# Two transformer blocks on one core: the first block's attention bias built by VectorE and GpSimd together

## What is computed

```python
def swa_bias_and_mask(positions, rel_bias):
    bucket = t5_bucket(pq[..., :, None] - pk[..., None, :])     # 32 buckets
    bias = rel_bias[bucket].astype(jnp.float32).reshape(b, nb, WINDOW, 2 * WINDOW, SWA_KV_HEADS, SWA_GROUP)
    ...

scores = jnp.einsum('bnqhgd,bnkhd->bnqkhg', qb, kk).astype(jnp.float32) * (SWA_HEAD_DIM ** -0.5) + bias
scores = jnp.where(mask, scores, NEG_INF)
```

## Time and profile before

| what | value |
|---|---|
| median of 3 runs | 2380.89 us (2378.52 to 2381.33) |
| the profiled execution | 2379.98 us |
| its span, from the first to the last instruction | 2378.1 us |
| PE, DVE, ACT, POOL busy | 2193.1, 991.6, 532.3, 3.6 us |
| granted clock of PE, mean | 0.968 of full speed |
| DVE busy in the first 250 us | 222 us |

### The profile page before, as it was taken

The page is one execution under the profiler, slowest core; times in us unless marked ns, Lnnn a source line. Parts: engine busy times, 40 slices in busy tenths (PEclk is TensorE's granted clock), DMA queues, the critical chain, the costliest instruction groups (busy, mean ns, idle before and its releaser), DMA issues.

```text
span 2378.1 us, 30893 instructions
## 1 busy us (share of the span) xinstructions
PE 2193.1 (92%) x12840; PEld 1510.0 (63%) x12840; DVE 991.6 (42%) x2028; ACT 532.3 (22%) x963; POOL 3.6 (0%) x11
## 2 busy tenths in 40 slices
PE   7999889998999889997999899999997799999996
PEld 6877579997877679997987644334334544334333
DVE  7899535552158335557447512111112511111112
ACT  2112104430113204334234211111112211111111
POOL 0000000000000000000000000000000000000000
PEclk9999999999999999998999899999999899999999
DMA  6445633453445733442220799999996399999993
GB/s 254 154 165 212 280 144 140 149 190 130 169 177 213 307 117 142 166 186 99 107 83 25 287 425 428 428 428 428 428 428 291 128 424 428 429 428 429 428 427 158
DMA packets 43770, 621.95 MB, mean 262 GB/s; under 512 B 4864, under 2 KB 4864, under 8 KB 5664
## 3 DMA queue, kind: packets, MB, share of 16 engines
q1 hardware_dynamic: 34416, 489.94, 50.9%
q10 hardware_dynamic: 8640, 125.83, 12.4%
q0 software_dynamic: 624, 4.92, 0.5%
HBM read 619.62 MB, written 1.05 MB: 261 GB/s over the span
## 4 chain that ended last, share of the span: by engine, by line
PE 64%; DMA 21%; DVE 11%; issue 2%; ACT 1%; SPq 0%; ACTq 0%; DVEq 0%
PE bank L549 19%; PE bank L1136 11%; DMA ring<-in_experts 11%; DMA arena<-in_experts 10%; PE bank L1158 4%; DVE wide L1729 3%; PE bank L742 3%; PE bank L743 3%; PE bank L744 3%; PE sums L744 3%; PE sums L743 3%; PE sums L742 3%; PE sums L549 2%; PE bank L870 2%; DVE arena L1756 2%; PE bank L871 2%
## 5 line engine op out<-in xcount | busy, mean ns | idle before, releaser
L549 PE MATMUL bank<-h,ring 128*128 128x256 f32 x1600 | 358.4, 385 | 15.1 <-DVE h L1654 12.1
L549 PEld LDWEIGHTS bank<-h,ring 128*128 128x128 f32 x1600 | 306.1, 193 | 65.0 <-DVE h L1654 12.9
L1158 PE MATMUL bank<-ring,wide 128*64 128x512 f32 x1024 | 233.8, 598 | 0.0
L2383 DVE TENSOR_TENSOR wide<-bank,wide 128x256 f32<-128x256 f32 x64 | 27.2, 425 | 420.1 <-ACT wide L1551 420.1
L1952 DVE TENSOR_TENSOR ring_split<-ring,arena_split 128x2048 fp32r<-128x2048 f32 x64 | 143.8, 2288 | 110.6 <-ACT arena_split L1387 110.5
L2391 DVE SCALAR_TENSOR_TENSOR scratch_split<-bank,small,wide_split 128x512 fp32r<-128x512 f32 x64 | 48.0, 750 | 272.3 <-ACT wide_split L1563 272.3
L742 PE MATMUL bank<-h_split,arena_split 128*128 128x256 f32 x512 | 146.7, 286 | 15.0 <-DVE ring_split L1952 15.0
L743 PE MATMUL bank<-scratch_split,arena_split 128*128 128x256 f32 x512 | 146.3, 286 | 0.0
L744 PE MATMUL bank<-h_split,ring_split 128*128 128x256 f32 x512 | 146.3, 286 | 0.0
L742 PE MATMUL sums<-smax_split,arena_split 128*128 128x256 f32 x512 | 144.9, 283 | 0.0
L743 PE MATMUL sums<-smax_split,arena_split 128*128 128x256 f32 x512 | 144.9, 283 | 0.0
(11 more groups left out here) (331 smaller groups left out, 3468.3 us busy)
## 6 DMA issues: line engine op xcount, KB each, us to landing
ring<-in_stream SPq DMA_DIRECT2D x100, 2048.0 KB, 7.8
ring<-in_experts SPq DMA_DIRECT2D x98, 2048.0 KB, 22.9
arena<-in_experts SPq DMA_DIRECT2D x34, 2048.0 KB, 24.3
ring<-in_experts ACTq DMA_DIRECT2D x30, 2048.0 KB, 14.1
arena<-in_experts ACTq DMA_DIRECT2D x30, 2048.0 KB, 14.0
wide<-in_na_bias POOLq DMA_DIRECT2D x1, 1536.0 KB, 8.6
arena<-in_consts POOLq DMA_DIRECT2D x1, 1088.0 KB, 5.3
x<-in_tokens SPq DMA_DIRECT2D x1, 1024.0 KB, 6.3
```

Of the source, the lines that this page charges most:

```text
L549: mm = pe.matmul(dst, a, b, start=(first and i == 0), stop=(i == len(terms) - 1))
L1158: mm = pe.matmul(banks[2][64 * half:64 * half + 64, :], M["turned"][:, e % 2, at:at + 64], w[:, k, 512 * half:512 * half + 512], start=(k ...
```

## The change

DVE keeps heads 0, 4, 1 and 5, the ones used in units 8 to 11. POOL builds heads 2, 6, 3 and 7, used in units 12 to 15, in this order, each head through all its 31 steps before the next. POOL has no fused multiply-add in this code: a step is a comparison times delta into `scratch` 4 or 5, then an addition to the head, each waiting for the instruction before. POOL begins when DVE has seeded all heads (`bias_begun`), and DVE waits, ahead of the scores of a unit whose head is POOL's, for that head's last addition (`bias_built`). The comparison of each step stays on DVE as well.

```diff
+VECTOR_HEADS, POOL_HEADS = (0, 4, 1, 5), (2, 6, 3, 7)
...
+            S.wait(pool, "bias_begun", 0)
+            for hd in POOL_HEADS:
+                v = flat2(wbias[:, hd])
+                for b in range(1, N_BUCKETS):
+                    step = scratch[:, 4 + S.count.get("bias_built", 0) % 2, :]
+                    if S.count.get("bias_built", 0) > 1:
+                        pool.wait_ge(S.sem("bias_built"), S.count["bias_built"] - 1)
+                    S.give(pool.tensor_scalar(step, flat2(A["away"]), float(thresholds[b - 1]), A["delta"][:, b * HEADS + hd:b * HEADS + hd + 1],
+                                              ALU.is_ge, ALU.mult), "bias_step", hd, b)
+                    S.wait(pool, "bias_step", hd, b)
+                    if b > 1:
+                        S.wait(pool, "bias_built", hd, b - 1)
+                    S.give(pool.tensor_tensor(v, v, step, ALU.add), "bias_built", hd, b)
             S.wait(pool, "x_added", 1, "mlp")
...
                 for hd in range(HEADS):
                     v = flat(wbias[:, hd])
                     ins = dve.tensor_scalar(v, v, A["delta"][:, hd:hd + 1], None, ALU.add)
-                link(ins)
...
+                give_link(ins, "bias_begun", 0)
...
-                    for hd in range(HEADS):
+                    for hd in VECTOR_HEADS:
                         v = flat(wbias[:, hd])
                         ins = dve.scalar_tensor_tensor(out=v, in0=reached, scalar=A["delta"][:, b * HEADS + hd:b * HEADS + hd + 1],
                                                        in1=v, op0=ALU.mult, op1=ALU.add)
...
                     hd = sink_of(u)
+                    if l == 0 and hd in POOL_HEADS:
+                        S.wait(dve, "bias_built", hd, N_BUCKETS - 1)
```

More of the change, by code:

```diff
@@ L378, in two_blocks_kernel @@
         loggam = small[:, 0:8]
+        thresholds = bucket_thresholds()
         def norm_col(i, s, which, k):
@@ L1714, in first_steps @@
                     ins = dve.tensor_scalar(v, v, A["delta"][:, hd:hd + 1], None, ALU.add)
-                link(ins)
-            thresholds = bucket_thresholds()
+                give_link(ins, "bias_begun", 0)
             steps = iter(range(1, N_BUCKETS))
```

## The result

The changed kernel is slower: median 2439.23 us of 4 runs (2435.69 to 2451.73) against 2380.26, a ratio of 1.0243 (95% interval 1.0212 to 1.0274), or +58 us. Its profiled execution took 2435.69 us, +55.7 against that of before.

What follows compares the result with a forecast made beforehand. DVE and PE were taken to run neck and neck. POOL's 109 us less 28 in free time put 81 on DVE; minus 49 saved, +32 on 2379.98 gave 2412.0 us, whole range 2375 to 2455.

Steps and rivals of the forecast that it cites:

- the forecast's mechanism: While POOL builds bias, its instructions and DVE's two-operand ones take full turns; +32 us at unit 8, kept to the end.
- The ledger of PE and DVE: Layer 0, units 8 to 15: 49 us less on DVE move the end by only 3.3 us, if nothing else changes.
- the fixed taps: Twelve convolution taps per unit from unit 8 on, with the softmax, keep DVE at 7.83 us a unit.
- The coupling: Up to unit 8: of POOL's 109 us, 28 fit free DVE time, 81 fall on DVE; less 49 saved, +32 us.
- PE's waits for DVE between 113 and 194 us: Sign of the forecast: such waits appear in that stretch if turns are taken, none before the change.
- The threshold of 0.20 us a POOL instruction: Loss on DVE per POOL instruction, over 248 of them, at which the 49 us removed are used up.
- The price of a POOL step: One head's comparison (0.33 us) and addition (0.55) on POOL: 0.88 us, bounds 0.66 to 1.30, about 1.1 with waits.
- "near 224" with turns: Sign: POOL's end is near 224 us under the forecast, 170 without coupling, 264 if DVE goes first.
- the due pace of 1.70 us: POOL's 124 steps, last due at unit 15 at 245.2 us, leave 211.3 / 124 = 1.70 us a step.
- POOL alone too slow: Rival, chance 0.04: POOL late from 1.70 us a step; at 2.2 head 7 is 62 us behind, +58, 2438 us.
- DVE goes first: Rival, chance 0.10: POOL only gets gaps, DVE isn't slowed, head 7 is late ahead of unit 15; +15.5, 2395.5 us.
- No coupling: Rival, chance 0.29: POOL's work costs DVE nothing that matters, DVE waits for PE before unit 9; -3.3, 2376.7 us.

Runs made afterwards that it cites:

- two runs without a wait: Changed kernel with only heads 3 and 7 on POOL: 1.0023, +5.5 us; changed kernel with POOL's comparison replaced by product and sum with constants: 1.0033, +7.9 us.
- two-head run: Changed kernel with only heads 3 and 7 on POOL and six heads on DVE: ratio 1.0023, +5.5 us (+2.9 to +8.1).
- full-DVE run: Kernel before, DVE with all eight heads, plus POOL's 248 instructions beside it on spare tiles: ratio 1.0287, +68 us.

## Why the prediction was right or wrong

- **Direction and range** held: slower, 2439 in 2375 to 2455. The direction rests on the forecast's mechanism, for the kernel is slower by coupling alone too (+5.5 and +7.9 in the two runs without a wait). That the size came out near is partly luck: the point, 2412, was 27 us short, and most of the +58 came from a wait that the forecast didn't have.
- **The ledger of PE and DVE** held. 49 us off DVE were worth 5.0 (3.3 forecast, in the interval), and the named cap, the fixed taps, was the cap: moved forward, the gain is 11.
- **The coupling** was right in kind and too high in size. 81 us were to fall on DVE by unit 8; 33 did, and 52 in all. Two terms were off. The loss is 0.45 us a step to unit 8, and 0.54 with DVE full all the time, under the 0.65 that 81 / 124 makes (0.44 an addition and 0.13 a comparison when each runs alone). And at its real pace POOL had made some 73 of its 124 steps by unit 8, so it went on taking time from DVE in units 8 to 14. At unit 8 the changed kernel stood at +0, where +32 was forecast, and PE's waits for DVE between 113 and 194 us, a sign named for the forecast, did not come. The threshold of 0.20 us a POOL instruction was the useful number: the pair costs 0.27.
- **The price of a POOL step is the term that failed.** Taken 0.88 us, bounds 0.66 to 1.30, from memsets, and about 1.1 with the waits; measured 1.86 with nothing beside it, and 2.05 with the waits. The addition was 0.72 against my 0.55, near enough. The comparison was 1.14 against 0.33. I costed an instruction by the elements it passes, with a row of another operation, and on POOL the operation is the price. My upper bound took half the memset's rate, and its 0.75 for the addition doesn't follow from that: two operands in turn at 1.67 ns an element make 0.97, and the bound 1.52. Even so it lies under 1.86, since the comparison lasts more than three times the 0.33 of one pass. So POOL's end, "170" alone and "near 224" with turns, became 303, and the due pace of 1.70 us, worked out correctly, was missed by every step.
- **The rival "POOL alone too slow"** at 2.2 us a step gave 2438 and had a chance of 0.04. It was the mechanism of the end: DVE's 18.9 us of coupling lie under POOL's 270 us, and without them DVE would only have waited longer, for a POOL that needs until 287 by itself. Counted from the seeding, 2.05 us a step makes POOL some 40 us late, and the 0.13 us by which DVE slows its step add 16: together the 55.7 of the two executions. It should have had several times that chance: the pace stood at 1.1 against 1.70 on rows of an operation that was not the added one.
- **DVE goes first** is refuted: beside additions turns are one for one, and DVE is the one that waits. **No coupling** is refuted by the two-head run (+5.5, interval above nought) and by the full-DVE run.
- The trace agrees with the rule named from the Trainium skill, SBUF — State Buffer, section Who interferes with whom, in who disturbs whom: two-operand DVE instructions beside POOL reads, one-operand fast ones beside memsets too, two-operand ones not beside memsets (475 to 486 ns). The size does not agree: that section says "for the whole instruction" of the two-port modes, and the prediction took it for two-operand instructions too; an addition of 0.72 to 0.79 us would then hold DVE that long, and it held it 0.46.

## What to carry to other kernels

An elementwise operation moved from DVE to POOL has two prices: POOL's own time against the due time, and what it takes from DVE while it runs; measure both for that very operation before counting anything as hidden. Here the first made nearly all of the +58: with a cheaper first instruction and the same loss on DVE it was +8. If the second exceeds what leaves DVE (here 0.44 us an addition against 0.395 us a multiply-add), no split beside a full DVE can be expected to pay. And where two engines are both full, ask what the next one allows: the 49 us taken from DVE were worth 5.

## What the runs showed of the hardware

- On POOL, 128x256 f32 with nothing beside it, a comparison with product takes 1.14 us and an addition of two tensors 0.72. Beside a working DVE a product with sum took 0.45 (0.51 between additions), a copy 0.42, a single product 0.85 and a comparison with product by constants 1.19 (1.07 at least). DVE's comparison of that size takes 0.29.
- DVE two-operand instructions and POOL's two-tensor additions take strict turns: eight multiply-adds in 6.96 us instead of 3.25, the longest single one 949 ns instead of 487. POOL's addition grows by 0.07 us only. Beside POOL's comparisons it is the other way round: they grow from 1.14 to 1.44 us on average, DVE's multiply-adds from 478 to 510 ns.
- POOL memsets leave DVE's two-operand instructions alone (largest of 248: 486 ns) and stretch its 0.29 us one-operand ones to 0.38 on average (median 0.294, longest 0.69).
- DVE instructions that read the accumulators keep their time beside POOL: 275 to 291 ns in the changed kernel, 280 to 285 before.
